# Experts' weights: four gate/up pieces of the next expert in a buffer of their own, copied into place, and 2 MB transfers

## The chip, the cores and the metric

The kernel runs on one core of a Trainium2 chip. The metric is the device time of one execution in microseconds, the median of several runs. All data is float32.

## The reference

Two layers of a network run on 512 tokens of width 1024. The first has a state-space mixer, a Fourier mixer and then a mixture of 32 experts, the second has attention, a gated recurrence and a dense feed-forward part. The change touches the experts alone:

```python
logits = (tok @ w_router + b_router)
top_logit, top_idx = lax.top_k(logits, TOP_K)            # 4 of 32 experts for each token
top_w = jax.nn.softmax(top_logit, axis=-1)
...
def expert_block(args):
    xe, e = args
    gu = xe @ w_gate_up[e] + b_gate_up[e]                # 1024 x 2048 for each expert: 8 MB
    gate = jnp.minimum(gu[:, :D_FF], SWIGLU_LIMIT)
    up = jnp.clip(gu[:, D_FF:], -SWIGLU_LIMIT, SWIGLU_LIMIT)
    act = (up + 1.0) * gate * jax.nn.sigmoid(SWIGLU_ALPHA * gate)
    return act @ w_down[e] + b_down[e]                   # 1024 x 1024 for each expert: 4 MB
```

Each token's four results are weighted by `top_w` and added. The 32 experts have 384 MB of weights, and each weight is needed once for each block of rows that its expert has.

## The kernel before

**Units.** The tokens of an expert are packed into units, which alternate between 32 rows (even units, `s = 0`) and 64 rows (odd units, `s = 1`). Two units make a turn of the loop (`PERIOD` = 96 rows). This input has 52 units in 26 turns, and an expert has one, two or three units, one after the other. Which expert a unit has is only known on the chip; a table `expert_of` says it (entry u + 1 for unit u, counted in the order in which the experts are worked off), and `first_unit` and `expert_at` give each expert's first unit and number.

**Weights.** Six slots of 16 KB in each partition hold one expert. A load is 1 MB (8 KB in each partition, half a slot). Gate/up weights are 16 pieces in 8 loads (slots 0 to 3), down weights are 8 pieces in 4 loads (slots 4 and 5). There is one semaphore for each of the 12 loads. There is no second copy: a half slot can be loaded again only when its last reader is through, and for an expert with several units that is in its last unit.

**SP (lines 1595 to 1605)** issues all these loads in one order. For each expert q with first unit u: eight gate/up loads, load i after piece 2i + 1 of unit u - 1; two small bias loads; four down loads, load i after down piece 2i + 1 in the turn of unit u (that product belongs to unit u - 1, see below). SP doesn't wait for a load to land; it waits only for the buffers.

**TensorE (lines 2752 to 2801)** does for each unit: gate/up pieces 0 to 7 (0 to 3 in a 64-row unit); transposes of the activations of the unit before (`turn_act`); pieces 8 and 9 (4 and 5); all eight down pieces of the unit before; the rest of the pieces, and in a 64-row unit transposes of the next tokens (`turn_x`) before piece 8 and at its end. Before each even piece it waits for the load that holds it.

**VectorE (lines 3721 to 3744)** waits for the biases of the unit, spreads them, waits for piece 15, and computes `gate`, `gate_min`, `up`, `up_clip`, `times` and `act`, with the sigmoid on ScalarE between. **GpSimd (lines 4110 to 4116)** once a turn waits for the end of the 64-row unit and gathers the rows of a later turn by an indirect DMA. **ScalarE** takes results out of PSUM and stores them.

`Steps` counts the steps of an engine on one semaphore: `at(name, u)` is its value once that step of unit u is done, `before(name, u)` that of unit u - 1.

Of the kernel before, what the change touches and what calls it, by code (L numbers as in the profile page):

```python
# [47 lines left out]
NE = 32  # L48
# [5 lines left out]
PART = D // TILES[0]  # L54
# [9 lines left out]
LOADS = GU_LOADS + DN_PIECES // 2  # L64
PIECE = 2 * 512
# [24 lines left out]
class Steps:  # L90
# [15 lines left out]
    def at(self, name, it=0):  # L106
        return it * self.n + (self.first + self.order.index(name) + 1)
# [45 lines left out]
def program(nc, io):  # L153
# [36 lines left out]
    def sem(name):  # L190
        return nc.alloc_semaphore(name)
# [10 lines left out]
    def row(w, i):  # L202
        return w[i] if isinstance(i, int) else w[bass.ds(i, 1)].rearrange("a p f -> p (a f)")
# [722 lines left out]
    def from_h(c, l, k):  # L926
# [127 lines left out]
                         "first_unit"] + [f"{n}{t}" for t in range(TT) for n in ("first_at", "first_pick")] + ["expert_of", "token_u", "y_row",  # L1054
# [9 lines left out]
    area = Area(AFTER_ROUTE, BACK_TABLES)  # L1064
# [3 lines left out]
    up = [area(f"up{s}", [P, s + 1, PART]) for s in range(2)]  # L1068
    sig = [area(f"sig{s}", [P, s + 1, PART]) for s in range(2)]
    aT = [area(f"aT{s}", [P, 2 * (s + 1), P]) for s in range(2)]  # L1070
    area = Area(AFTER_TABLES, AFTER_H)
    b_few = [area(f"b_few{s}", [P, s + 1, 2 * PART]) for s in range(2)]
    area = Area(AFTER_X1 + 36 * 1024)
    b_there = area("b_there", [P, 1])
    exp_loaded = w_loaded + [sem(f"exp_loaded{i}") for i in range(6, 18)]
    exp_first = loads + [0] * 12
# [7 lines left out]
    moe_xT_act = Steps(sem("moe_xT_act"), ["half0", "half1"], 1, ahead=True)  # L1084
    end_pe = Steps(sem("end_pe"), ["aT", "down"])
# [7 lines left out]
    AT_BANK, Y_BANK_OF = [3, 5], [7, 6]  # L1093
    s_gate_zero = sem("s_gate_zero")
# [362 lines left out]
    def _(sp):  # L1457
# [108 lines left out]
        def load_piece(i, e):  # L1566
            sp.dma_start(slot[i // 2][:, i % 2 * 2 * PIECE:(i % 2 + 1) * 2 * PIECE], row(io["w_exp"], e * LOADS + i)).then_inc(exp_loaded[i], 16)

# [5 lines left out]
        for i in range(GU_LOADS, LOADS):  # L1574
            load_piece(i, 0)
# [5 lines left out]
        for i in range(2, GU_LOADS):  # L1581
            load_piece(i, 0)
        sp.wait_ge(s_few, 2)
# [3 lines left out]
        moe_dn.open(sp)  # L1587
        route_dve.after(sp, "first_unit")
# [662 lines left out]
    def _(pe):  # L2251
# [500 lines left out]
        def turn(i, last_turn=False):  # L2752
            for s in range(2):
# [4 lines left out]
                def gate_up(pieces):  # L2758
                    for piece in pieces:
                        k, t = piece // 2, piece % 2  # L2760
                        if piece % 2 == 0:
                            pe.wait_ge(exp_loaded[piece // 2], e * 16 + (exp_first[piece // 2] + 16))
                        for h in range(2):
                            at = piece % 4 * PIECE + h * 512
                            half, tile = divmod(2 * t + h, TILES[s])
                            rows, first = UNIT_ROWS[s], UNIT_AT[s]
                            last = pe.matmul(GATE_PS[s][tile * rows:(tile + 1) * rows, half, :], xT_blk[:, k, first:first + rows],  # L2767
                                             slot[piece // 4][:, at:at + 512], start=(k == 0), stop=(k == KD - 1))
                        moe_gu.done(last, f"gu{piece}")
# [21 lines left out]
                for k in range(DN_PIECES):  # L2791
                    if k % 2 == 0:
                        pe.wait_ge(exp_loaded[GU_LOADS + k // 2], e_before * 16 + 16)
                    moe_dn.done(down(k, 1 - s), f"dn{k}")
# [301 lines left out]
    def _(dve):  # L3096
# [572 lines left out]
        step("y_row", dve.tensor_scalar(row_f[:], row_f[:], float(UNIT_ROWS[1]), None, ALU.add))  # L3669

# [19 lines left out]
        def last_rows(u):  # L3690
            last_dve.done(dve.tensor_scalar(last_from[:], n_started[:], -float(PERIOD), -float(UNIT_ROWS[1]), ALU.mult, ALU.add), "from")
# [29 lines left out]
        def turn(i, last=False):  # L3721
            for s in range(2):
# [7 lines left out]
                moe_dve.done(dve.stream_shuffle(b_row[s][:], b_few[s][:], [0] * 32), "spread")  # L3730
                dve.wait_ge(moe_dve.sem, moe_dve.at("spread", u))
# [12 lines left out]
                moe_dve.done(dve.tensor_tensor(gate[s][:], gate[s][:], sig[s][:], ALU.mult), "act")  # L3744

# [302 lines left out]
    def _(pool):  # L4048
# [60 lines left out]
        n = i_last + 1  # L4109
        with pool.Fori(0, i_last - 1) as i:  # L4110
# [5 lines left out]
            gather(token_now[:])  # L4116

# [3 lines left out]
        pool.wait_ge(exp_loaded[LOADS - 1], 16 * NE)  # L4121
# [144 lines left out]
def lay_out(x, c, ctx, c_ctx, w_mod, b_mod, norm1_w, norm2_w, w_in, conv_w, conv_b, dt_bias, a_log,  # L4266
# [58 lines left out]
    out["w_exp"] = np.concatenate([gu, dn], 1).reshape(NE * LOADS, P, 2 * PIECE)  # L4325
# [30 lines left out]
```

## Time and profile before

| what | value |
|---|---|
| median of 3 timed runs | 3032.16 us (3027.61 to 3032.35) |
| profiled execution, span | 3025.3 us; the profile gives no other time of it |
| TensorE matmuls busy | 2841.0 us, 94% |
| VectorE busy | 1377.2 us, 46% |
| ScalarE busy | 846.3 us, 28% |
| GpSimd busy | 303.8 us, 10% |
| read from HBM, written | 593.89 MB, 36.44 MB |
| expert weight loads | 384 of 1024 KB, median 11.4 us from issue to landing |
| expert stage (first to last of its TensorE work) | 992 to 2074 us |

In the page's 40 slices (75.6 us each) the experts are slices 14 to 28. There the DMA engines' digits are 8 and 9 and they move 310 to 411 GB/s, while TensorE's digits are 8 and 9 as in most of the span. A matmul counts as busy from its start to its modelled end, so TensorE's share says little about how near it is to its limit. The time from issue to landing of a load holds the time in which it stands behind others.

### The profile page before, as it was taken

To read this page: it belongs to the slowest core of one execution; us is meant where nothing else is said; L and a number is where in the kernel's file an instruction comes from. 1 tells how busy PE (TensorE), PEld (TensorE's weight loads), DVE (VectorE), ACT (ScalarE), POOL (GpSimd) and SP (SyncE) were. 2 spreads that over 40 slices of the span, in tenths; PEclk is the share of its full clock that TensorE was granted. 3 is DMA by queue.
4 is the path that set the end of the run, shared out by engine and by line. 5 is a ranking of instruction groups with operands and counts; after the bars stand their busy time and mean duration, and the time that the engine had idled before them with its cause. 6 is when DMAs were issued, how large, how long until landed. Compare 5 with 4: busy or idle time off the path is not lost.

```text
span 3025.3 us, 41220 instructions
## 1 busy us (share of the span) xinstructions
PE 2841.0 (94%) x15088; PEld 1753.1 (58%) x15089; DVE 1377.2 (46%) x2323; ACT 846.3 (28%) x1661; POOL 303.8 (10%) x291
## 2 busy tenths in 40 slices
PE   8999999999999978888989898879999999999999
PEld 5665656746888422222323232226877888888887
DVE  5768678644455211112112121124674786555551
ACT  4547365501212211111211121113243544211100
POOL 0101011310001000000000000003111553000000
PEclk9999999999999988999989998989999999999999
DMA  5433425355124899979798989997120222122111
GB/s 226 160 112 132 150 95 205 154 199 194 67 89 166 337 410 405 409 316 402 313 404 348 387 328 410 411 411 290 56 115 17 92 81 98 35 89 86 61 65 60
DMA packets 137826, 634.03 MB, mean 210 GB/s; under 512 B 12848, under 2 KB 55728, under 8 KB 77040
## 3 DMA queue, kind: packets, MB, share of 16 engines
q1 hardware_dynamic: 110832, 562.65, 47.3%
q0 software_dynamic: 10112, 35.66, 3.6%
q10 hardware_dynamic: 16768, 34.17, 3.1%
q8 instruction: 76, 1.25, 0.2%
q14 instruction: 38, 0.31, 0.0%
HBM read 593.89 MB, written 36.44 MB: 208 GB/s over the span
## 4 chain that ended last, share of the span: by engine, by line
PE 79%; DMA 10%; DVE 4%; ACT 3%; issue 2%; POOL 1%; SPq 0%; ACTq 0%; DVEq 0%; POOLq 0%
PE ps L340 27%; PE ps L2767 17%; PE ps L2747 9%; PE ps L2317 9%; DMA slot<-in_w_exp 8%; PE ps L279 3%; PE ps L2464 2%; DMA w_modT<-in_w_modT 2%; PE ps L3030 2%; PE ps L2473 2%; PE ps L3002 1%; PE ps L2738 1%; PE ps L2985 1%; PE ps L2256 1%; ACT decay L1818 1%
## 5 line engine op out<-in xcount | busy, mean ns | idle before, releaser
L2767 PE MATMUL ps<-slot,xT_blk 128*32 128x512 f32 (+1 forms) x3328 | 615.7, 638 | 137.7 <-DMA slot<-in_w_exp 137.3
L2767 PEld LDWEIGHTS ps<-slot,xT_blk 128*32 128x32 f32 (+1 forms) x3328 | 159.3, 128 | 497.3 <-issue 307.5
L2747 PE MATMUL ps<-slot,aT 128*32 128x256 f32 (+1 forms) x2528 | 286.5, 454 | 0.0
L3729 DVE MEMSET b_there<- 128x1 f32 x52 | 3.1, 59 | 494.7 <-DMA b_few<-in_b_gu 482.2
L2747 PEld LDWEIGHTS ps<-slot,aT 128*32 128x32 f32 (+1 forms) x2528 | 111.3, 119 | 183.8 <-issue 152.4
L3733 DVE TENSOR_TENSOR gate<-ps,b_row 128x256 f32<-128x256 f32 (+1 forms) x52 | 29.0, 558 | 344.1 <-PE ps L2767 344.1
L340 PE MATMUL ps<-in_t,in_s 128*128 128x264 f32 x528 | 124.8, 387 | 0.5 <-issue 0.5
L2464 PE MATMUL ps<-hT,slot 128*128 128x512 f32 x256 | 120.7, 604 | 2.2 <-ACT zT L1763 2.1
L2317 PE MATMUL ps<-h_sum,w_sum 128*128 128x384 f32 (+1 forms) x384 | 120.2, 460 | 0.0
L1980 ACT ACTIVATE y_row<-ps 128x512 f32<-128x512 f32 (+1 forms) x52 | 25.5, 490 | 333.2 <-PE ps L2747 333.2
L340 PEld LDWEIGHTS ps<-in_t,in_s 128*128 128x128 f32 x528 | 100.5, 190 | 17.8 <-DVE in_s L429 0.9
L279 PE MATMUL ps<-gate_yT,slot 128*128 128x512 f32 x256 | 110.0, 593 | 0.0
L1983 ACT ACTIVATE aT<-ps 128x512 f32<-128x512 f32 (+1 forms) x53 | 26.1, 492 | 272.9 <-PE ps L2738 272.9
L2317 PEld LDWEIGHTS ps<-h_sum,w_sum 128*128 128x128 f32 x384 | 72.5, 190 | 40.1 <-issue 1.9
L3231 DVE SCALAR_TENSOR_TENSOR conv_b<-raw,g_conv,conv_b 128x510 f32<-128x510 f32 (+1 forms) x112 | 66.8, 633 | 46.7 <-ACT conv_b L1736 45.6
L340 PE MATMUL ps<-xnT,in_w 128*128 128x264 f32 x352 | 85.5, 387 | 0.0
L279 PEld LDWEIGHTS ps<-gate_yT,slot 128*128 128x128 f32 x256 | 48.8, 191 | 60.7 <-issue 59.4
L2004 ACT ACTIVATE sig<-gate 128x256 f32<-128x256 f32 (+1 forms) x52 | 27.2, 523 | 195.7 <-DVE gate L3735 195.6
L1818 ACT ACTIVATE decay<-sum_here,g_small 128x128 f32<-128x128 f32 x256 | 78.1, 387 | 13.6 <-PE ps L2473 13.6
L2317 PE MATMUL ps<-hT,slot 128*128 128x384 f32 (+1 forms) x256 | 81.1, 462 | 0.0
L4115 POOL TENSOR_TENSOR token_there<-cst 128x1 f32<-128x1 f32 x24 | 4.6, 192 | 755.0 <-PE ps L2733 755.0
L279 PE MATMUL ps<-xnT,slot 128*128 128x264 f32 x352 | 80.3, 386 | 0.0
(572 smaller groups left out, 4984.9 us busy)
## 6 DMA issues: line engine op xcount, KB each, us to landing
slot<-in_w_exp SPq DMA_DIRECT2D x384, 1024.0 KB, 11.4
in_w<-in_w_ffn SPq DMA_DIRECT2D x22, 1024.0 KB, 4.8
expert_rows<-zero SPq DMA_DIRECT2D x4, 4608.0 KB, 24.3
slot<-in_w_xbc SPq DMA_DIRECT2D x8, 2048.0 KB, 8.2
sum_here<-sum_rows ACTq DMA_DIRECT2D x32, 512.0 KB, 3.7
w_modT<-in_w_modT POOLq DMA_DIRECT2D x32, 512.0 KB, 3.9
rnn_w<-in_w_rnn SPq DMA_DIRECT2D x16, 1024.0 KB, 4.9
out_w<-in_w_ffn_out SPq DMA_DIRECT2D x8, 1408.0 KB, 7.5
```

Source lines behind the costliest of these rows:

```text
L279: last = pe.matmul(self.bank(j, part), self.layout(slot[s], m, k), self.rhs(k, part), start=(k == 0), stop=(k == self.k - 1))
L340: last = pe.matmul(like(out, right), lhs[:, k, :], right, start=(start and k == 0), stop=(k == self.kh - 1), skip_group_check=not start)
L1818: last = act.activation(decay[j % 2][:, h, :], sum_here[j % 2][:, h, :], ACT.Abs, bias=g_small[:, MINUS_SUM, t, d, h:h + 1])
L2256: pe.matmul(ps[:, bank, 0:256], ident, cst[:, 0:256], start=True, stop=True)
L2317: last = pe.matmul(out, left[:, k, :], right(k), start=(start and k == 0), stop=(k == KD // 2 - 1), skip_group_check=not start)
L2464: last = pe.matmul(ps[:, 3, :], slot[SSD_SLOT[s, "z"][0]][:, (k * 4 + m) * P:(k * 4 + m + 1) * P], hT[:, k, 0:SEQ], start=(k == 0), stop=( ...
L2473: last = pe.matmul(ps[half, Y_BANK + h // 2, t * P:(t + 1) * P], left[:, h * HD:(h + 1) * HD], right[:, h, :], start=first, stop=True, ski ...
L2738: last = pe.transpose(ps[:, AT_BANK[s], c * P:(c + 1) * P], acts[:, c * P:(c + 1) * P], ident)
L2747: last = pe.matmul(ps[j * rows:(j + 1) * rows, Y_BANK_OF[s], 0:width], aT[s][:, 2 * half + c, tile * rows:(tile + 1) * rows], slot[4 + k / ...
L2767: last = pe.matmul(GATE_PS[s][tile * rows:(tile + 1) * rows, half, :], xT_blk[:, k, first:first + rows], slot[piece // 4][:, at:at + 512], ...
L3030: last = pe.matmul(ps[:, 2 * (j % 4) + p, 0:H2], slot[j // 4][:, (k * 4 + j % 4) * P:(k * 4 + j % 4 + 1) * P], attnT[:, k, p * H2:(p + 1) ...
L3231: last = dve.scalar_tensor_tensor(out=acc[:, lo:hi], in0=raw_tile(m)[:, lo + off:hi + off], scalar=g_conv[:, m, k:k + 1], in1=acc[:, lo:hi ...
```

## The change

- A new area of 32 KB in each partition at the top of SBUF (`AHEAD_AT`) holds the last four gate/up loads (4 to 7, pieces 8 to 15, 4 MB) of the next expert. Slots 2 and 3 hold those of the present expert, as before. Several small buffers move to make room. `span` is one tensor from slot 2 to the end of SBUF, so that source and place are offsets in it.
- At the end of each unit these four are copied to slots 2 and 3 for the next unit: from the new area if the next unit has another expert, else onto themselves (`held_from` is the offset, `TO_AHEAD` or 0). VectorE does this behind `act` of the unit: copies 4 to 7 after a 32-row unit, 5 to 7 after a 64-row unit. There GpSimd does copy 4, after piece 9 of that unit. A copy is 128x2048 elements.
- TensorE waits for the copies instead of loads 4 to 7.
- SP's order for each expert: gate/up loads 0 to 3 and the biases as before; wait for copies 4 and 5 of its first unit, then loads 4 and 5 of the next expert in one transfer of 2 MB; wait for copy 7, then loads 6 and 7 in another; then the down weights in two transfers of 2 MB, after down pieces 3 and 7. The second expert's four start after the first piece of unit 0.
- Weights in HBM lie in two tensors, 1 MB rows for loads 0 to 3, 2 MB rows for the others. Three small instructions in the routing make `held_from`. Semaphores of the later layers are numbered anew.

```diff
+        def load_pair(i, e, at=0):
+            into = span[:, at + (i - 4) * 2 * PIECE:at + (i - 2) * 2 * PIECE] if i < GU_LOADS else slot[i // 2][:]
+            sp.dma_start(into, row(io["w_two"], e * (LOADS // 2 - 2) + (i // 2 - 2))).then_inc(exp_loaded[i], 16)
...
-        with sp.Fori(1, NE) as q:
-            u = sp.value_load(first_unit[0:1, bass.ds(q, 1)], min_val=1, max_val=UNITS)
-            e = sp.value_load(expert_at[0:1, bass.ds(q, 1)], min_val=0, max_val=NE - 1)
-            for i in range(GU_LOADS):
+        def load_gate_up(e, u):
+            for i in range(GU_LOADS - AHEAD):
                 sp.wait_ge(moe_gu.sem, moe_gu.before(f"gu{2 * i + 1}", u))
                 load_piece(i, e)
             sp.wait_ge(moe_dve.sem, moe_dve.before("spread", u))
             load_bias(e)
-            for i in range(DN_PIECES // 2):
-                sp.wait_ge(moe_dn.sem, moe_dn.before(f"dn{2 * i + 1}", u + 1))
-                load_piece(GU_LOADS + i, e)
+
+        def load_down(e, u):
+            for i in range(0, DN_PIECES // 2, 2):
+                sp.wait_ge(moe_dn.sem, moe_dn.before(f"dn{2 * i + 3}", u + 1))
+                load_pair(GU_LOADS + i, e)
+
+        e_first = sp.value_load(expert_at[0:1, 1:2], min_val=0, max_val=NE - 1)
+        moe_gu.after(sp, "gu0")
+        for i in range(GU_LOADS - AHEAD, GU_LOADS, 2):
+            load_pair(i, e_first, TO_AHEAD)
+        with sp.Fori(1, NE - 1) as q:
...
+            load_gate_up(e, u)
+            sp.wait_ge(moe_copy4.sem, moe_copy4.before("copy4", u))
+            sp.wait_ge(moe_copies.sem, moe_copies.before("copy5", u))
+            load_pair(4, e_next, TO_AHEAD)
+            sp.wait_ge(moe_copies.sem, moe_copies.before("copy7", u))
+            load_pair(6, e_next, TO_AHEAD)
+            load_down(e, u)
...
@@ TensorE, gate_up
-                        if piece % 2 == 0:
+                        if piece % 2 == 0 and piece < 2 * (GU_LOADS - AHEAD):
                             pe.wait_ge(exp_loaded[piece // 2], e * 16 + (exp_first[piece // 2] + 16))
+                        elif piece == 8:
+                            pe.wait_ge(moe_copy4.sem, moe_copy4.before("copy4", u))
+                        elif piece % 2 == 0:
+                            pe.wait_ge(moe_copies.sem, moe_copies.before(f"copy{piece // 2}", u))
...
@@ VectorE, behind "act"
+                if more:
+                    for k in range(s, AHEAD):
+                        dve.wait_ge(exp_loaded[landed(4 + k)], e_next * 16 + (exp_first[landed(4 + k)] + 16))
+                        copied = dve.tensor_copy(held(k), span[:, bass.ds(from_at + k * 2 * PIECE, 2 * PIECE)])
...
@@ GpSimd
+        def copy_4(i):
+            u = 2 * i + 2
...
+            pool.wait_ge(moe_gu.sem, moe_gu.at("gu9", u - 1))
+            pool.wait_ge(exp_loaded[4], e * 16 + (exp_first[4] + 16))
+            moe_copy4.done(pool.tensor_copy(held(0), span[:, bass.ds(from_at, 2 * PIECE)]), "copy4")
...
             pool.tensor_copy(token_now[:], token_u[:, bass.ds(i + 2, 1)]).then_inc(s_now, 1)
+            copy_4(i)
             pool.wait_ge(moe_xT_pe.sem, moe_xT_pe.at("half1", i))
```

## Rows read from the trace of the kernel before

**Rows 1.** The page's costliest group: busy, mean ns | idle before it, releaser.

```profile
L2767 PE MATMUL ps<-slot,xT_blk 128*32 128x512 f32 (+1 forms) x3328 | 615.7, 638 | 137.7 <-DMA slot<-in_w_exp 137.3
```

**Rows 2.** Windows: busy us by engine (instructions), PEclk, DMA share, GB/s.

```profile
992.00:2074.00 1082.00, 943.93 (x6244) 310.45 (x6244) 213.38 (x485) 192.96 (x411) 37.59 (x76) 0.92 0.95 380
1093.00:1107.00 14.00, 8.92 (x30) 2.56 (x34) 0.00 (x0) 0.38 (x1) 0.00 (x0) 0.61 1.02 424
1322.00:1337.00 15.00, 15.00 (x132) 5.85 (x128) 2.14 (x4) 2.49 (x9) 1.19 (x2) 1.00 0.04 9
1438.00:1453.00 15.00, 15.00 (x128) 5.77 (x124) 2.21 (x5) 2.64 (x10) 1.27 (x2) 1.00 0.03 9
1654.00:1664.00 10.00, 10.00 (x60) 3.04 (x58) 1.97 (x6) 2.30 (x3) 0.18 (x1) 1.00 0.12 26
1766.00:1777.00 11.00, 11.00 (x64) 3.32 (x62) 2.04 (x6) 2.30 (x3) 0.18 (x1) 1.00 0.11 25
```

**Rows 3.** Timeline of SP, expert stage: start, length, issues merged.

```profile
993.48 14.21 SPq L1567 DMA_DIRECT2D slot<-in_w_exp  x8
1014.16 27.67 SPq L1567 DMA_DIRECT2D slot<-in_w_exp  x12
1048.30 12.27 SPq L1567 DMA_DIRECT2D slot<-in_w_exp  x12
1178.05 26.97 SPq L1567 DMA_DIRECT2D slot<-in_w_exp  x12
1308.24 42.38 SPq L1567 DMA_DIRECT2D slot<-in_w_exp  x12
1634.59 46.41 SPq L1567 DMA_DIRECT2D slot<-in_w_exp  x12
```

**Rows 4.** Chain of work, two units and the last load: start, length.

```profile
1397.98 19.72 DMA slot<-in_w_exp
1435.72 1.87 PE ps L2767 x8
1437.59 3.59 PE ps L2747 x64
1443.53 7.02 PE ps L2767 x32
1451.02 3.57 PE ps L2767 x32
2053.47 16.10 DMA slot<-in_w_exp
```

**Rows 5.** Timeline of DVE, "gate" and "act" of three units.

```profile
1431.86 0.42 DVE L3733 TENSOR_TENSOR gate<-ps,b_row 128x256 f32<-128x256 f32 x1 [2.63 <-PE ps L2767]
1450.59 0.69 DVE L3733 TENSOR_TENSOR gate<-ps,b_row 128x512 f32<-128x512 f32 x1 [14.44 <-PE ps L2767]
1453.66 0.69 DVE L3744 TENSOR_TENSOR gate<-gate,sig 128x512 f32<-128x512 f32 x1
1466.00 0.42 DVE L3733 TENSOR_TENSOR gate<-ps,b_row 128x256 f32<-128x256 f32 x1 [10.33 <-PE ps L2767]
1468.01 0.42 DVE L3744 TENSOR_TENSOR gate<-gate,sig 128x256 f32<-128x256 f32 x1
```

**Rows 6.** Groups of DVE by shape: busy us, mean ns | idle before.

```profile
L3738 DVE TENSOR_SCALAR up<-up 128x512 f32<-128x512 f32 x26 | 11.5, 443 | 0.9
L3738 DVE TENSOR_SCALAR up<-up 128x256 f32<-128x256 f32 x26 | 7.6, 294 | 0.9
```

**Rows 7.** The same view of GpSimd.

```profile
L4066 POOL TENSOR_TENSOR x_dt<-x_tok,g_small 128x2048 f32<-128x2048 f32 x4 | 15.8, 3952 | 52.6 <-PE ps L2473 52.6
L4100 POOL MEMSET b_few<- 128x1024 f32 x1 | 1.0, 952 | 0.0
```

**Rows 8.** DMA issues: count, KB each, median us to landing.

```profile
in_w<-in_w_ffn SPq DMA_DIRECT2D x22, 1024.0 KB, 4.8
slot<-in_w_gf SPq DMA_DIRECT2D x2, 2048.0 KB, 7.9
```

More of the change, by code:

```diff
@@ L1063, in program @@
     y_row = [area(f"y_row{s}", [P, s + 1, PART]) for s in range(2)]
-    area = Area(AFTER_ROUTE, BACK_TABLES)
+    up = [area(f"up{s}", [P, s + 1, PART]) for s in range(2)]
+    sig = [area(f"sig{s}", [P, s + 1, PART]) for s in range(2)]
+    assert area.next <= STAGE + KD * SEQ * 4
+    area = Area(AFTER_H, AFTER_ROUTE)
     b_row = [area(f"b_row{s}", [P, s + 1, 2 * PART]) for s in range(2)]
@@ L1067, in program, with landed @@
     gate = [area(f"gate{s}", [P, s + 1, PART]) for s in range(2)]
-    up = [area(f"up{s}", [P, s + 1, PART]) for s in range(2)]
-    sig = [area(f"sig{s}", [P, s + 1, PART]) for s in range(2)]
     aT = [area(f"aT{s}", [P, 2 * (s + 1), P]) for s in range(2)]
+    meta_x = area("meta_x", [P, KD, N_META])
+    square_meta = area("square_meta", [P, KD, N_META])
+    b_there = area("b_there", [P, 1])
+    AHEAD_AT = END // 32 * 32 - AHEAD * SLOT_BYTES // 2
+    assert area.next <= AHEAD_AT
+    area = Area(AHEAD_AT)
+    area.next += AHEAD * SLOT_BYTES // 2
+    assert area.next <= END
+    HELD_AT = FREE + (GU_LOADS - AHEAD) * SLOT_BYTES // 2
+    span = at("span", [P, (END // 32 * 32 - HELD_AT) // 4], HELD_AT)
+    TO_AHEAD = (AHEAD_AT - HELD_AT) // 4
     area = Area(AFTER_TABLES, AFTER_H)
     b_few = [area(f"b_few{s}", [P, s + 1, 2 * PART]) for s in range(2)]
[L1073 to L1076, printed above, removed]
+    exp_loaded = w_loaded + [sem(f"exp_loaded{i}") for i in range(6, 16)]
+    exp_first = loads + [0] * 10
+    def landed(piece):
+        return piece if piece < GU_LOADS - AHEAD else piece - piece % 2
     TURN_AT, DOWN_AT = [8, 4], [10, 6]
@@ L1093, in program, with held @@
     AT_BANK, Y_BANK_OF = [3, 5], [7, 6]
+    def held(k, at=0):
+        return span[:, at + k * 2 * PIECE:at + (k + 1) * 2 * PIECE]
     s_gate_zero = sem("s_gate_zero")
@@ L1573, in _ @@
         four_out.pe.all(sp)
-        for i in range(GU_LOADS, LOADS):
-            load_piece(i, 0)
+        for i in range(GU_LOADS, LOADS, 2):
+            load_pair(i, 0)
         w_o.pe.after(sp, "p4_1")
@@ L2760, in gate_up @@
                         k, t = piece // 2, piece % 2
-                        if piece % 2 == 0:
+                        if piece % 2 == 0 and piece < 2 * (GU_LOADS - AHEAD):
                             pe.wait_ge(exp_loaded[piece // 2], e * 16 + (exp_first[piece // 2] + 16))
+                        elif piece == 8:
+                            pe.wait_ge(moe_copy4.sem, moe_copy4.before("copy4", u))
+                        elif piece % 2 == 0:
+                            pe.wait_ge(moe_copies.sem, moe_copies.before(f"copy{piece // 2}", u))
                         for h in range(2):
                             at = piece % 4 * PIECE + h * 512
+                            weights = slot[piece // 4]
+                            if piece >= 2 * (GU_LOADS - AHEAD):
+                                weights, at = span, at + (piece // 4 * 4 - 2 * (GU_LOADS - AHEAD)) * PIECE
                             half, tile = divmod(2 * t + h, TILES[s])
@@ L2767, in gate_up @@
                             last = pe.matmul(GATE_PS[s][tile * rows:(tile + 1) * rows, half, :], xT_blk[:, k, first:first + rows],
-                                             slot[piece // 4][:, at:at + 512], start=(k == 0), stop=(k == KD - 1))
+                                             weights[:, at:at + 512], start=(k == 0), stop=(k == KD - 1))
                         moe_gu.done(last, f"gu{piece}")
@@ L2801, in turn @@
                     gate_up(range(DOWN_AT[s], GU_PIECES))
+        for i in range(GU_LOADS - AHEAD, GU_LOADS, 2):
+            pe.wait_ge(exp_loaded[i], exp_first[i] + 16)
         with pe.Fori(0, i_last) as i:
@@ L3730, in turn @@
                 moe_dve.done(dve.stream_shuffle(b_row[s][:], b_few[s][:], [0] * 32), "spread")
+                more = not (s and last)
+                if more:
+                    e_next = dve.value_load(expert_of[0:1, bass.ds(u + 2, 1)], min_val=0, max_val=NE - 1)
+                    from_at = dve.value_load(held_from[0:1, bass.ds(u + 1, 1)], min_val=0, max_val=TO_AHEAD)
                 dve.wait_ge(moe_dve.sem, moe_dve.at("spread", u))
@@ L3744, in turn @@
                 moe_dve.done(dve.tensor_tensor(gate[s][:], gate[s][:], sig[s][:], ALU.mult), "act")
+                if more:
+                    for k in range(s, AHEAD):
+                        dve.wait_ge(exp_loaded[landed(4 + k)], e_next * 16 + (exp_first[landed(4 + k)] + 16))
+                        copied = dve.tensor_copy(held(k), span[:, bass.ds(from_at + k * 2 * PIECE, 2 * PIECE)])
+                        if k == 0:
+                            moe_copy4.done(copied, "copy4")
+                        else:
+                            moe_copies.done(copied, f"copy{4 + k}")
         with dve.Fori(0, i_last) as i:
```

58 lines of the change are left out of this document (41 added, 17 removed).

## The prediction

> **What bounds the kernel now.** I read the page first: TensorE matmuls are busy 94% of the span, and the costliest group of waits behind them is on the expert weights, 137 us of idle TensorE before the gate/up matmuls [rows 1]. So the stage to look at is the experts', 992 to 2074 us. The windows view tells which resource is full there [rows 2]: over the whole stage the DMA engines are busy 0.95 of the time at 380 GB/s; where TensorE waits for weights (1093 to 1107) they stand at 1.02 and 424 GB/s, which is as full as they get, with transfers of 1 MB. A transfer of 1 MB (1.049 MB in bytes) then takes 2.47 us. The stage is bound by DMA, and TensorE's waits are the consequence. What can be won is only the time in which the DMA engines stand idle, and that is in four places: 15, 15, 10 and 11 us, together 51 us, at a share of 0.03 to 0.12 [rows 2].
>
> The SP queue's timeline says why just there [rows 3]. A burst of 12 issues is four down loads of one expert, then eight gate/up loads of the next, which wait for that expert's last unit. Its length gives the expert's units: 12 to 14 us is one unit (14 such bursts), 27 us two units (26.97 for the 3 that begin on a 32-row unit, 27.67 for the 9 that begin on a 64-row unit), 42.38 or 46.41 us three units (2 and 2). The four idle places lie in the four three-unit bursts. Two-unit experts leave the DMA engines no idle time now, because the eight gate/up loads of the next expert are released one by one all through the last unit.
>
> **The DMA ledger of before.** First issue 993.48, last landing 2053.47 + 16.10 = 2069.57 [rows 3, 4]: 1076.1 us for 31 experts. Off this go the 51 us idle and four restarts of 2.3 us (a lone 1 MB load lands after 4.8 us [rows 8], 2.47 are its bytes): 60 us. What is left is 1016 us, so D = 32.8 us for the 12 MB of an expert, the stores and gathers that share the engines included.
>
> **What the change does to the queue.** Order on SP for an expert e with first unit u becomes: gate/up loads 0 to 3 of e (released in unit u-1, as now); then the wait for copy 4 and 5 of unit u and a 2 MB load of the next expert's pieces, the wait for copy 7 and the second 2 MB; then the down weights in two 2 MB loads. The copies of unit u run on VectorE behind "act" of unit u-1, that is after the last matmul of u-1 and the whole SwiGLU chain. So for each expert all traffic stops at one point until the previous expert's last unit is computed, evaluated and copied. Before, no such point existed: gate/up loads 4 to 7 needed only the piece of the slot they fill. Between two such points lie exactly 12 MB. Call T the landing of gate/up load 3 of e. Behind T the queue holds 12 MB more (ahead pieces, down, next loads 0 to 3), so the DMA engines run dry at T + 32.8. The next issue comes at T + TensorE's way to the end of e's last unit + the VectorE chain + one copy (5; after a 64-row unit GpSimd does copy 4) or two (4 and 5).
>
> Terms, all from rows:
> - TensorE. In the trace a load 3 lands at 1397.98 + 19.72 = 1417.70, and the two units behind it (32, then 64 rows) end at 1450.55 [rows 4]: 32.8 us; the first alone ends near 1431.8, 14.1 us. Each further unit is read off the "gate" instructions that wait for a unit's end, at 1431.86, 1450.59, 1466.00 [rows 5]: 18.7 us for 64 rows, 15.4 for 32. An expert that begins on a 64-row unit needs load 2 (T - 2.5) for pieces 4 and 5, and from there to the unit's end it is 1450.55 - 1435.72 = 14.8 [rows 4]: T + 12.3.
> - VectorE chain: 1466.00 to 1468.43 is 2.4 us; 1450.59 to 1454.35 is 3.8 us [rows 5].
> - A copy of 128x2048 on VectorE is not in the trace. The one-source operation takes 294 ns for 256 and 443 ns for 512 elements [rows 6], a slope of 0.58 ns: 1.3 us. The two-source one ("gate", 0.42 and 0.69 us [rows 5]) has 1.06 ns: 2.3 us. The copy has one source in SBUF and so has the first; I take 1.3. Below, nothing; above, 2.3.
> - Restart of an empty queue with a 2 MB load: 7.9 us lone [rows 8] less 4.9 for its bytes, 3.0 us. Bounds 1.5 (half of it hidden) and 3.3.
>
> Idle time per expert (path less 32.8):
> - one unit: 14.1 + 2.4 + 2.6 + 3.0 = 22.1, below 32.8: none.
> - two units, 32 rows first: 32.8 + 3.8 + 1.3 + 3.0 = 40.9: 8.1 us, x3 = 24.
> - two units, 64 rows first: 12.3 + 15.4 + 2.4 + 2.6 + 3.0 = 35.7: 2.9 us, x9 = 26.
> - three units, 32 rows first: 14.1 + 18.7 + 15.4 + 2.4 + 2.6 + 3.0 = 56.2: 23.4 us, x2 = 47.
> - three units, 64 rows first: 12.3 + 15.4 + 18.7 + 3.8 + 1.3 + 3.0 = 54.5: 21.7 us, x2 = 43.
>
> Together 140 us idle against 60 before: +80. About 5 us come back, since stores and gathers, which D holds as a share, now move some of their bytes in idle time. The sum is +75 us.
>
> **The other parts.** VectorE's copies delay TensorE nowhere while their weights are there: after a 32-row unit they end 2.4 + 5.2 = 7.6 us on, while the next unit reaches piece 8 after pieces 0 to 7, down and transposes, about 11.7 us [rows 4]; after a 64-row unit three end 3.8 + 3.9 = 7.7 us on and piece 10 comes after 12.7 us. Behind the copies on VectorE stand the bias spread (0.7 to 1.3 us) and the next "gate", 15 us away. At 2.3 us a copy piece 8 still gets copy 4 in time. GpSimd's copy 4 starts at piece 9 of the 64-row unit, 5.3 us before its end, and is bounded by 1.0 us (memset, 1024 elements) and 3.95 us (two sources, 2048 elements) [rows 7]; it is off the path either way. The gather behind it on GpSimd waits for the unit's end anyway. Transfers of 2 MB instead of two of 1 MB: bytes and the rate are the same, zero; SP issues 8 instead of 12 loads, each far shorter than its transfer, zero. The start: the first expert's ahead pieces load from 992.6 on instead of 993.5, zero, but put 10 us before the loads of unit 1, which belongs to the 12 MB cycles already counted. Three routing instructions of some 0.2 us: nothing.
>
> A lone load shows a fixed part of 2.3 us for 1 MB, and full windows of 1 MB loads show none [rows 2, 8]. The Trainium skill (DMA: Bandwidth & Descriptors, section Anatomy of one DMA) gives about 2.0 us plus bytes over 436 GB/s for a transfer (fitted on the GpSimd path), 4.4 us for this one, and by it larger transfers pay. If each transfer of a full queue cost its 2.0 us, four fewer for each of 31 experts would save 248 us, an estimate from that page; the 424 GB/s of 1 MB loads speak against it.
>
> **The sum.** The profile has a span of 3025.3 us and gives no time of its own around it; the timed runs, 3027.6 to 3032.4, lie 2 to 7 us above it. The stage grows from 1082 to 1157 us, all else stays: 3025 + 75 = 3100 in span, 3032 + 75 = 3107 us in the median.
>
> **Rivals.**
> - Faster: the prefetch closes the four idle places and opens none. All 60 us come back: 2972. It decides at the point where the issue waits for copies end before the queue is dry, a path below 32.8 us for two-unit experts: the 64-row-first ones miss it by 2.9, which a restart hidden behind the running transfer would give back, the 32-row-first ones by 8.1; the three-unit ones can't reach it, since one expert's 12 MB is all that the buffers take. For it: the slots' wait does start 4 MB earlier in a long expert. Against: the same 12 MB lie between two waits. 0.09.
> - Full queues gain from fewer, larger transfers, 2.0 us for each of 124: 3107 - 248 = 2859, faster; for it only the lone load's fixed part, against it [rows 2]. 0.02.
> - The loss is small: two-unit experts lose nothing, because their next issue is hidden behind the running transfers, and a restart costs 1.5. Then the three-unit experts idle 90 - 6 = 84 us against 60, +24: 3056; with stores and gathers filling all of that, 3032. 0.07, half of it within 0.2%.
> - Copies at 2.3 us: 3 + 18 + 4 + 2 = 27 copies lie on the path, +27: 3134. By the skill (SBUF — State Buffer, section SBUF: two separate sides) VectorE in a two-port mode and GpSimd exclude each other for whole instructions; no row shows them together, and it would act in the same direction. 0.17.
> - The forecast, 3107: 0.65.
>
> **Range and chances.** Low end: 3 us off each of 16 restarts (48) is 3059, and the small loss ends at 3056: 3055. High end: copies at 2.3 and the low clock after longer waits, about 1 us on each of the 16 (a 32-row unit's transposes and pieces 8, 9 take longer behind the wait): 3150. Slower by over 0.2% (6 us, what a measurement can tell): 0.65 + 0.17 + 0.035 = 0.855, within 0.2%: 0.03, faster: 0.115.
>
> **What would show it.** In the changed profile: SP waits for VectorE's copies, longest in two-unit experts that begin with 32 rows and in three-unit experts; DMA share of the stage about 0.89 instead of 0.95, with gaps ahead of the ahead pieces of some 3, 8 and 22 us; VectorE copies near 1.3 us; TensorE still waiting on DMA at the first piece of an expert, and almost never on a copy. I am wrong if the share rises, if SP's wait for the copies ends before the queue is dry, or if 12 MB take clearly more or less than 32.8 us.

## The result

The changed kernel takes 3104.5 us (median of 4 runs, 3101.2 to 3107.2) against 3029.9 us before in the same comparison: a ratio of 1.0251, 95% interval 1.0236 to 1.0267 (the record's own; the quotient of the two medians would be 1.0246). It is slower by 2.5%; the forecast was 3107, the range 3055 to 3150. The profiled execution took 3104.6 us with a span of 3102.8 us, 77.5 more than before's span.

The page of the kernel after (groups: busy us, mean ns | idle before, releaser; DMA issues: count, KB, median us to landing). The one group of [rows 1] is now two, since pieces 8 to 15 are read through `span`:

```profile
L2821 PE MATMUL ps<-slot,xT_blk 128*32 128x512 f32 (+1 forms) x1664 | 331.4, 671 | 208.3 <-DMA slot<-in_w_exp 207.9
L2794 PE MATMUL ps<-slot,aT 128*32 128x256 f32 (+1 forms) x2528 | 288.8, 455 | 8.1 <-DMA slot<-in_w_two 8.0
L2821 PE MATMUL ps<-span,xT_blk 128*32 128x512 f32 (+1 forms) x1664 | 286.2, 602 | 0.0
L3812 DVE COPY span<-span 128x2048 f32 x179 | 207.5, 1219 | 0.0
L4189 POOL COPY span<-span 128x2048 f32 x25 | 47.2, 1890 | 727.9 <-PE ps L2821 727.9
slot<-in_w_exp SPq DMA_DIRECT2D x128, 1024.0 KB, 14.0
span<-in_w_two SPq DMA_DIRECT2D x64, 2048.0 KB, 10.7
```

TensorE's idle time for gate/up weights rose from 137.7 [rows 1] to 208.3 us, and 8.1 us for down weights are new: together 79 us, about what the span grew by. It never waits for a copy (0.0 before the `span` matmuls). The VectorE copies cost 207.5 us of VectorE's time, most of it beside other work.

The windows view of the kernel after (columns as in [rows 2]; the five engines are TensorE, its weight loads, VectorE, ScalarE and GpSimd). I call a stop a stretch in which the queue has run dry, or nearly, and the next load is still held back, and I call experts 32-first or 64-first by the rows of their first unit. The rows are the whole expert stage, a stretch in which TensorE waits, then a stop in an expert of two units beginning with 64 rows, one in an expert of two beginning with 32, one in an expert of three beginning with 32 and one in an expert of three beginning with 64, and the last expert:

```profile
994.00:2157.00 1163.00, 946.40 (x6244) 309.52 (x6236) 414.03 (x663) 194.14 (x412) 90.84 (x105) 0.90 0.89 355
1106.00:1120.00 14.00, 7.99 (x34) 2.41 (x38) 3.40 (x6) 0.38 (x1) 0.00 (x0) 0.65 1.01 424
1050.00:1060.00 10.00, 10.00 (x98) 3.96 (x96) 6.12 (x8) 1.18 (x4) 0.00 (x0) 1.00 0.68 250
1218.00:1232.00 14.00, 14.00 (x90) 4.58 (x88) 7.59 (x12) 3.44 (x7) 1.76 (x3) 1.00 0.54 188
1345.00:1386.00 41.00, 40.71 (x318) 14.20 (x314) 19.55 (x31) 7.95 (x18) 3.33 (x4) 1.00 0.51 187
1703.00:1742.00 39.00, 37.29 (x254) 12.46 (x252) 15.93 (x26) 7.53 (x16) 3.83 (x5) 1.00 0.55 184
2126.00:2150.00 24.00, 23.39 (x158) 10.32 (x154) 7.99 (x16) 2.46 (x5) 2.11 (x2) 0.93 0.61 238
```

The same view of the kernel before, wider than in [rows 2] so that the restarts are inside: one of the two stops of each kind, and the last expert. (The page's DMA digits of the slices 14 to 28 there are 7 to 9, at 290 to 411 GB/s, and not only 8 and 9; the 7s of slices 18 and 20, at 316 and 313 GB/s, are two of these stops.)

```profile
1318.00:1345.00 27.00, 27.00 (x196) 9.55 (x194) 6.07 (x13) 5.23 (x13) 1.44 (x3) 1.00 0.42 154
1650.00:1668.00 18.00, 18.00 (x110) 5.59 (x110) 4.46 (x13) 3.70 (x6) 0.18 (x1) 1.00 0.33 105
2050.00:2072.00 22.00, 21.38 (x158) 10.05 (x148) 6.15 (x14) 3.85 (x7) 1.87 (x2) 1.00 0.84 339
```

The stage grew from 1082 to 1163 us, and its share fell from 0.95 to 0.89, while a full stretch still moves 424 GB/s. So the loss is time in which DMA doesn't run at that rate, and a window tells how much: its length times (1 - GB/s / 424). That holds idle time and restart together, as the terms of the forecast did. Before, the four stops lose 17.2, 16.9, 13.5 and 12.8 us, 60 in all. After:

| stop | count | one, lost us | all | forecast |
|---|---|---|---|---|
| one unit | 14 | none seen | 0 | 0 |
| two units, 64 rows first | 9 | 3.3 to 4.7 | 36 | 26 |
| two units, 32 rows first | 3 | 7.8, 7.2, 7.4 | 22 | 24 |
| three units, 32 rows first | 2 | 22.9, 22.9 | 46 | 47 |
| three units, 64 rows first | 2 | 22.1, 22.2 | 44 | 43 |
| last expert (before 4.4) | 1 | 10.5 | +6 | 0 |

The stops lose 148 us, 88 more than before; with the last expert 94. The stage shows 81, so 13 us come back in stores and gathers that now move in idle time.

The place of a stop is seen in three views of the kernel after, here for the expert of two units that begins with 32 rows. The chain of work (start, length):

```profile
1162.49 25.41 DMA slot<-in_w_exp
1199.12 10.27 DMA slot<-in_w_two
1213.72 7.02 PE ps L2821 x32
```

The timelines of VectorE and of SP behind it:

```profile
1220.79 0.69 DVE L3797 TENSOR_TENSOR gate<-ps,b_row 128x512 f32<-128x512 f32 x1 [10.81 <-PE ps L2821]
1223.87 0.69 DVE L3808 TENSOR_TENSOR gate<-gate,sig 128x512 f32<-128x512 f32 x1
1224.47 3.49 DVE L3812 COPY span<-span 128x2048 f32 x3
1225.87 2.61 SPq L1590 DMA_DIRECT2D span<-in_w_two  x2
```

Load 3 lands at 1187.90 (1162.49 + 25.41). The last unit of its expert ends at 1220.74, 32.8 us on. VectorE evaluates until 1224.47, the first copy ends near 1225.7, and SP issues the first ahead load at 1225.87 and the second after copy 7, some 2.3 us later (the row's 2.61 us run to the end of the second issue). The queue had held 12 MB behind load 3 and ran empty at the same time (the first of these windows; the other two belong to the expert of three units at 1345):

```profile
1219.00:1226.00 7.00, 7.00 (x58) 2.17 (x52) 4.97 (x8) 3.42 (x7) 1.27 (x2) 1.00 0.21 69
1348.00:1363.00 15.00, 14.71 (x116) 5.22 (x112) 3.77 (x6) 3.22 (x11) 3.15 (x3) 1.00 0.08 16
1376.00:1381.00 5.00, 5.00 (x24) 1.41 (x20) 4.79 (x8) 0.81 (x3) 0.00 (x0) 1.00 0.01 2
```

SP's waits (in all us, count, the longest) name who holds it. By its releasers L1644 is the wait for copy 4; the waits for copies 5 and 7 are counted at the issues, L1590:

```profile
SPq L1644 <- DVE span L3812: 120.9, 12, 11.8
SPq L1590 <- DVE span L3812: 156.9, 60, 7.9
SPq L1644 <- POOL span L4189: 11.6, 5, 2.3
```

### The profile page after: what moved, and what is told of

Read it like the earlier page. It is cut to its first block, busy times and chain, and to the rows that moved or that the text cites. A ratio compares the mean times of both kernels' runs of the same rounds, so it can differ in the third digit from the quotient of the medians.

```text
span 3102.8 us, 41967 instructions
## 1 busy us (share of the span) xinstructions
PE 2842.4 (92%) x15088; PEld 1747.3 (56%) x15089; DVE 1577.7 (51%) x2505; ACT 846.4 (27%) x1661; POOL 352.0 (11%) x317
## 4 chain that ended last, share of the span: by engine, by line
PE 76%; DMA 15%; DVE 3%; ACT 2%; issue 2%; SPq 1%; POOL 1%; ACTq 0%; DVEq 0%; POOLq 0%
PE ps L341 26%; PE ps L2821 13%; DMA slot<-in_w_exp 9%; PE ps L2364 9%; PE ps L2794 8%; PE ps L280 6%; DMA slot<-in_w_two 4%; PE ps L2511 2%; PE ps L3086 2%; PE ps L2520 2%; PE ps L3058 1%; PE ps L3041 1%; DMA slot<-in_w_mod 1%; PE ps L2785 1%; ACT decay L1865 1%
## 5 line engine op out<-in xcount | busy, mean ns | idle before, releaser
L2821 PE MATMUL ps<-slot,xT_blk 128*32 128x512 f32 (+1 forms) x1664 | 331.4, 671 | 208.3 <-DMA slot<-in_w_exp 207.9
L2821 PEld LDWEIGHTS ps<-slot,xT_blk 128*32 128x32 f32 (+1 forms) x1664 | 79.9, 131 | 404.0 <-DMA slot<-in_w_exp 254.9
L2821 PE MATMUL ps<-span,xT_blk 128*32 128x512 f32 (+1 forms) x1664 | 286.2, 602 | 0.0
L3812 DVE COPY span<-span 128x2048 f32 x179 | 207.5, 1219 | 0.0
L2821 PEld LDWEIGHTS ps<-span,xT_blk 128*32 128x32 f32 (+1 forms) x1664 | 79.4, 123 | 164.8 <-issue 161.9
L4189 POOL COPY span<-span 128x2048 f32 x25 | 47.2, 1890 | 727.9 <-PE ps L2821 727.9
```

The costliest lines, as they stand in the source:

```text
L3812: copied = dve.tensor_copy(held(k), span[:, bass.ds(from_at + k * 2 * PIECE, 2 * PIECE)])
L4189: moe_copy4.done(pool.tensor_copy(held(0), span[:, bass.ds(from_at, 2 * PIECE)]), "copy4")
```

## The experiments

Each is an edit of the kernel after, but for the one that says so. Times are medians, the ratio is to the kernel before in the same comparison.

**The copies' length.** In e2 VectorE's copies move 32 columns instead of 2048.

```diff
-copied = dve.tensor_copy(held(k), span[:, bass.ds(from_at + k * 2 * PIECE, 2 * PIECE)])
+copied = dve.tensor_copy(held(k)[:, 0:32], span[:, bass.ds(from_at + k * 2 * PIECE, 32)])
```

> The changed kernel with VectorE's copies cut to 32 columns each (so pieces 8 to 15 of later experts are multiplied mostly with old weights; GpSimd's copy stays whole): all waits and their places remain, only the length of a copy goes from 1.22 us to about 0.1. Theory A: 27 copies lie on the paths that empty the queue, 27 x 1.1 = 30 us less than the changed kernel: 3070 to 3080. Theory C (VectorE's 208 us of copies are the loss): all 75 us back, 3030. If copies are hidden altogether: 3104.

Measured: 3074.35 us, 1.0147 (1.0130 to 1.0164), in the range. The group of copies:

```profile
L3812 DVE COPY span<-span 128x32 f32 x179 | 22.9, 176 | 0.4 <-issue 0.4
```

Each is 1.04 us shorter (1.219 - 0.176). Pieces 8 to 15 of later experts are multiplied mostly with old weights. The forecast's 27 copies on the path make 28 us; the ratio fell by 0.0104, 31 us of 3030. Of 76 us lost (0.0251), 31 are the copies' own length. The other 45 stay although the copies take almost no time.

**The copies twice.** In e3b a second pass, times 1.0, follows each of VectorE's copies 5 to 7, and the waits are for that.

```diff
+moe_copies.done(copied, f"first{4 + k}")
+dve.wait_ge(moe_copies.sem, moe_copies.at(f"first{4 + k}", u))
+moe_copies.done(dve.tensor_scalar(held(k), held(k), 1.0, None, ALU.mult), f"copy{4 + k}")
```

> The changed kernel, and behind each of VectorE's copies 5, 6 and 7 a second pass over the copied 128x2048 in place (times 1.0), so that copy 5, 6 and 7 each take twice as long; copy 4 once. Theory A: one doubled copy, copy 5, lies ahead of the first ahead load in each of the 16 experts with two or three units, 16 x 1.3 = 21 us more: 3118 to 3132; the doubled 6 and 7 end within the 5 us that the first 2 MB take. Theory C (the loss goes with VectorE's busy time): 150 more passes of 1.2 us, 60 us more or all 180: 3165 and up. If copies are hidden: 3104.

Measured: 3146.54 us, 1.0398 (1.0380 to 1.0415): 0.0147 or 44 us above the kernel after. Both numbers of the expectation missed; mine, 3118 to 3132, counted one pass more at each of 16 stops. The windows and SP's timeline of this kernel, for the stops at 1345 and 1703 of the kernel after and the issue at 1225.87:

```profile
1353.00:1394.00 41.00, 40.99 (x317) 14.41 (x318) 29.56 (x37) 8.30 (x18) 4.42 (x4) 1.00 0.48 173
1728.00:1770.00 42.00, 38.75 (x252) 12.74 (x250) 24.12 (x33) 7.53 (x16) 4.02 (x5) 0.96 0.48 162
1229.32 5.13 SPq L1590 DMA_DIRECT2D span<-in_w_two  x2
```

These two stops lose 24.3 and 26.0 us instead of 22.9 and 22.1. SP's timeline tells where all of the 44 us are. The ahead loads before and at one 64-first stop, first in the kernel after and then in this one:

```profile
1241.08 2.61 SPq L1590 DMA_DIRECT2D span<-in_w_two  x2
1292.80 2.61 SPq L1590 DMA_DIRECT2D span<-in_w_two  x2
```

```profile
1244.53 5.28 SPq L1590 DMA_DIRECT2D span<-in_w_two  x2
1299.96 5.13 SPq L1590 DMA_DIRECT2D span<-in_w_two  x2
```

From one to the other it is 51.7 us in the kernel after and 55.4 here. Taken for all 16 stops, these stretches are longer by 24 us (nine 64-first experts of two units), 8 (three 32-first) and 12 (four of three units), 44 in all. One pass at each stop is in it as counted: the first ahead load comes 4.9 or 5.1 us behind the last unit's "gate" in the kernel after and 6.1 to 6.4 here, some 20 us in all. The other 24 arise behind the first ahead load, where the expectation had nothing. My reading, not tested by itself: the two ahead loads are now issued over 5.13 us, against 2.61. In the kernel after the second is in the queue well before the bytes of the first (4.9 us) are through; here it comes about as they end, so the passes between copies 5 and 7 count as well.

**The copies' place.** In e5 VectorE makes copies 4 to 6 ahead of the unit's SwiGLU, after pieces 9, 11 and 13 of its last unit have been read; only copy 7 stays behind `act`. The same copies and transfers.

```diff
+for k in range(s, AHEAD - 1):
+    dve.wait_ge(moe_gu.sem, moe_gu.at(f"gu{9 + 2 * k}", u))
+    copy(k)
...
-    for k in range(s, AHEAD):
+    copy(AHEAD - 1)
```

> The changed kernel with VectorE's copies 4, 5 and 6 moved ahead of the SwiGLU chain, each as soon as its pieces are through (pieces 9, 11, 13); copy 7 stays behind 'act'. Theory A (the DMA queue runs dry because the next ahead load waits for last unit + VectorE chain + copy): the paths get 6 to 7 us shorter, the gaps of two-unit experts go, those of three-unit experts shrink by 5 to 7: 50 to 74 us back, 3030 to 3055 us. Theory B (the loss is the size and order of the transfers, not the wait): about 3104. Theory C (VectorE's copies themselves are in the way of the work): no gain, since as many copies run, or worse, because they now stand ahead of the activation: 3104 or more.

Measured: 3050.25 us, 1.0079 (1.0062 to 1.0096), in the range of the first theory. VectorE's timeline and SP's waits of this kernel:

```profile
1206.65 1.25 DVE L3798 COPY span<-span 128x2048 f32 x1 [10.05 <-PE ps L2821]
1208.35 1.23 DVE L3798 COPY span<-span 128x2048 f32 x1 [0.45 <-PE ps L2821]
1209.87 0.69 DVE L3810 TENSOR_TENSOR gate<-ps,b_row 128x512 f32<-128x512 f32 x1 [0.29 <-PE ps L2821]
SPq L1644 <- DVE span L3798: 5.8, 12, 2.1
SPq L1590 <- DVE span L3798: 219.4, 48, 7.5
```

Two copies are done ahead of "gate" at 1209.87. SP's wait for copy 4, 120.9 us, is down to 5.8. Those for copies 5 and 7 rise from 156.9 to 219.4 us, since copy 7 still stands behind `act` and is now what SP stands at. Together they fall by 53 us, and 52 of the 76 us are back with every copy still made. So it is shown that the place of the copies behind SwiGLU is the larger part of the loss.

**The transfers' size.** e8 leaves the copies late and makes all loads 1 MB, each behind its own copy; e7 has early copies and 1 MB loads; e1 is the kernel before with the down weights in 2 MB loads.

```diff
-into = span[:, at + (i - 4) * 2 * PIECE:at + (i - 2) * 2 * PIECE] if i < GU_LOADS else slot[i // 2][:]
-sp.dma_start(into, row(io["w_two"], ...)).then_inc(exp_loaded[i], 16)
+for j in (i, i + 1):
+    wait(j)
+    into = held(j - 4, at) if j < GU_LOADS else slot[j // 2][:, j % 2 * 2 * PIECE:(j % 2 + 1) * 2 * PIECE]
+    sp.dma_start(into, row(io["w_two"], e * (LOADS - 4) + (j - 4))).then_inc(exp_loaded[j], 16)
```

> The changed kernel, copies where the change put them, but all loads of 1 MB, each released by its own copy or down pieces. With the run of early copies and 1 MB loads (ratio 1.0018) and early copies and 2 MB loads (1.0079) it makes the fourth corner. Theory A: the late place of the copies is the larger part and the 2 MB grain the smaller, and a late copy costs less where copy 4 alone releases the first load: 35 to 60 us above the kernel before, 3060 to 3090. If the grain matters only beside late copies: under 3050.

> The early copies as in the other run, and all loads of 1 MB again, each released by its own copy or down pieces. Theory A with grains (a 2 MB load is released by the later of its two halves and lands as a whole, some 2.5 us each time where the queue is near dry): 10 to 20 us below the early copies with 2 MB loads, 3025 to 3045. If the size of a transfer in a queue that is mostly full is nothing: the same as the early copies within 5 us.

The edit of e1, in the kernel before:

```diff
-for i in range(DN_PIECES // 2):
-    sp.wait_ge(moe_dn.sem, moe_dn.before(f"dn{2 * i + 1}", u + 1))
-    load_piece(GU_LOADS + i, e)
+for i in range(0, DN_PIECES // 2, 2):
+    sp.wait_ge(moe_dn.sem, moe_dn.before(f"dn{2 * i + 3}", u + 1))
+    load_pair(GU_LOADS + i, e)
```

> The kernel before with one part of the change alone: the down weights in two transfers of 2 MB instead of four of 1 MB, gate/up loads as before, no new buffer and no copies. If each transfer of a full queue had a fixed cost of 2.0 us (the Trainium skill, DMA: Bandwidth & Descriptors, section Anatomy of one DMA), 62 fewer would save 124 us: 2903. Theory A (no fixed cost in a full queue; a 2 MB load is released later and lands as a whole): the same to 12 us slower, 3027 to 3040. Theory B (the size is what costs the changed kernel its time): half or more of the 75 us, 3060 and up.

Measured: e8 3076.82 us, 1.0161 (1.0144 to 1.0178); e7 3033.91, 1.0018 (1.0008 to 1.0027); e1 3033.28, 1.0016 (1.0006 to 1.0025). All three are in their ranges. With the kernel after and e5 that gives, as loss against before:

| | 2 MB | 1 MB |
|---|---|---|
| copies behind `act` | +76 us | +49 us |
| copies 4 to 6 ahead of it | +24 us | +5 us |

(the ratio less 1, times 3030; by the intervals each is good to 3 to 5 us). The place is worth 52 and 43 us, the size 27 and 19, which is too near to call them different. The size is no cost of the transfer: 64 large ones for 128 small ones cost 5 us in before's order. What differs is the wait: the first ahead load in e8 waits for copy 4 alone. That is one copy less behind `act` of a 32-row unit, and behind a 64-row unit none of VectorE's, since GpSimd makes copy 4 during that unit. The windows of e8 at a 32-first and a 64-first stop:

```profile
1218.00:1232.00 14.00, 13.00 (x84) 3.72 (x76) 6.32 (x11) 4.31 (x7) 0.50 (x2) 1.00 0.82 321
1285.00:1301.00 16.00, 14.16 (x116) 5.40 (x112) 5.38 (x9) 2.50 (x9) 3.10 (x3) 1.00 0.99 407
```

They lose 3.4 and 0.6 us, against 7.8 and 3.8 in the kernel after.

**What the ahead area is worth.** In e4 there are no copies: SP waits only for the landing of the previous ahead load and TensorE for the landings. The values of pieces 8 to 15 are therefore not the right ones; traffic and matmuls are the same. e9 is that with 1 MB loads.

```diff
-sp.wait_ge(moe_copy4.sem, moe_copy4.before("copy4", u))
-sp.wait_ge(moe_copies.sem, moe_copies.before("copy5", u))
+sp.wait_ge(exp_loaded[4], q * 16 + (exp_first[4] + 16))
 load_pair(4, e_next, TO_AHEAD)
-sp.wait_ge(moe_copies.sem, moe_copies.before("copy7", u))
+sp.wait_ge(exp_loaded[6], q * 16 + (exp_first[6] + 16))
 load_pair(6, e_next, TO_AHEAD)
```

> The changed kernel without any copy (its gate/up pieces 8 to 15 are multiplied with the first expert's weights that stay in place; this is the part of the computation that it changes); TensorE waits for the landing of each expert's ahead loads instead, and SP issues the next ones as soon as the previous ones have landed, without waiting for a unit's end. All bytes are loaded in the same transfers and order. Theory A: the gaps behind units go, what is left are the waits for slots in three-unit experts, as before the change, and 2 MB grains: 3035 to 3055. If loading 4 MB ahead wins by itself and only the copies spoil it: under 3000. Theory B (size and order of transfers): still near 3100.

> As the run without copies (pieces 8 to 15 always with the first expert's weights in place, SP never waits for a unit's end ahead of the ahead loads), and all loads of 1 MB. It is the bound of what 4 MB more of look-ahead can give in this order of loads. The run without copies and with 2 MB loads had a ratio of 1.0024, and 1 MB loads took 0.0061 to 0.0090 off in the two pairs of runs; so if the grain is the rest of its loss: 0.994 to 0.998, 3010 to 3022 us, 4 MB of look-ahead are worth 6 to 18 us and the copies with early places eat them. If look-ahead is worth nothing here (the three-unit gaps keep their length, the last expert has nothing behind it): 1.000 to 1.002.

Measured: e4 3035.44 us, 1.0024 (1.0014 to 1.0034), at the low end of its range and not under 3000, where look-ahead would have brought it. e9 3033.26 us, 1.0010 (1.0001 to 1.0019), the expectation for an area worth nothing. So the area alone, with copies that cost nothing, saves nothing. The windows of e9, a three-unit expert and the last one:

```profile
1328.00:1343.00 15.00, 15.00 (x128) 5.79 (x124) 2.02 (x4) 2.33 (x8) 1.03 (x2) 1.00 0.04 9
2050.00:2076.00 26.00, 25.38 (x162) 10.84 (x160) 6.17 (x14) 2.52 (x6) 2.32 (x2) 0.89 0.64 248
```

The gap of 15 us in a three-unit expert stands as in [rows 2] (0.04, 9 GB/s), and so do the other three, at shares of 0.04, 0.14 and 0.24. Loads 0 to 3 still have to wait until the slots are free in the expert's last unit. My reading of it, from the order and not tested by itself: the queue behind load 3 is 4 MB longer, but the first unit can now be finished when load 3 is there and not load 7, also 4 MB earlier, so the two cancel. The traces agree. VectorE's timeline, the "gate" that waits for the end of that first unit, in the kernel before and in e9:

```profile
1316.01 0.42 DVE L3733 TENSOR_TENSOR gate<-ps,b_row 128x256 f32<-128x256 f32 x1 [2.42 <-PE ps L2767]
1322.18 0.42 DVE L3805 TENSOR_TENSOR gate<-ps,b_row 128x256 f32<-128x256 f32 x1 [13.05 <-PE ps L2819]
```

The gap begins near 1322 before and near 1328 in e9: both times 6 us behind this point. And the last expert has no ahead loads behind it: that window loses 10.8 us, in before 4.4.

**Another order.** In e6 the down weights stand ahead of the ahead pieces.

```diff
 load_gate_up(e, u)
+load_down(e, u)
 sp.wait_ge(moe_copy4.sem, moe_copy4.before("copy4", u))
...
-load_down(e, u)
```

> The changed kernel with the down weights of an expert loaded ahead of the next expert's ahead pieces. Theory A: SP's stop is then at down piece 3 of the expert's first unit, which comes 3 to 7 us later than the copies, and with it the ahead loads' stop: each of the 31 experts' cycles can only get longer, 3150 to 3210. Rival (the ahead pieces delay weights that are needed sooner, the down weights that TensorE waits for): down weights come earlier, 3060 to 3095.

Measured: 3206.53 us, 1.0593 (1.0575 to 1.0611), in the range. TensorE's group and SP's wait of this kernel:

```profile
L2821 PE MATMUL ps<-slot,xT_blk 128*32 128x512 f32 (+1 forms) x1664 | 343.1, 693 | 305.3 <-DMA slot<-in_w_exp 304.8 <-issue 0.4
SPq L1590 <- PE ps L2794: 752.5, 62, 34.2
```

The down slots are free later than the copies are made, and all that stands behind the down loads in the queue waits with them: 305 us of idle TensorE, against 208 in the kernel after. Which waiting load stands first decides more here than how much buffer there is.

No version beats the kernel before. The nearest, e9, e1 and e7, are 0.10, 0.16 and 0.18% above it.

## Why the prediction was right, step by step

- **Bound by DMA.** Right: share 0.89 as forecast, TensorE busy 943.9 [rows 2] and 946.4 us in the stage, its waits up by 79 us, and the rate of a full stretch unchanged at 424.
- **One stop per expert, 12 MB between two.** Right. SP stands at L1644 and L1590 on VectorE's copies (the first ahead load comes 4.9 us behind the "gate" of a 32-row unit and 5.1 us behind that of a 64-row unit; the forecast had 5.0 and 5.1), and e5 takes away 52 us by moving them. T + 32.8 for both the end of two units and the dry queue held where I looked (1220.7 and the window from 1219).
- **The stops' lengths.** 148 us against 140. The 64-first experts of two units lose 4.0 instead of 2.9 us each, +10 in all; the others are within 1 to 2 us as groups. The term that was too small is the first 64-row unit, T + 12.3. In six of the nine its "gate" comes at T + 13.3 to 14.2, together some 9 us more. TensorE's timeline at pieces 0 to 3 of such an expert (its T is 1259.0) and of one whose weights were there at once; then two windows of the first:

```profile
1251.51 5.75 PE L2821 MATMUL ps<-slot,xT_blk 128*64 128x512 f32 x16 [15.41 <-DMA slot<-in_w_exp]
1375.23 3.65 PE L2821 MATMUL ps<-slot,xT_blk 128*64 128x512 f32 x16
```

```profile
1252.00:1255.00 3.00, 3.00 (x10) 0.73 (x8) 0.00 (x0) 0.00 (x0) 0.00 (x0) 0.50 1.01 426
1257.00:1260.00 3.00, 3.00 (x24) 1.08 (x26) 0.55 (x3) 0.38 (x1) 0.00 (x0) 1.00 1.08 442
```

Behind a wait of 15.41 us TensorE's granted clock is 0.50 (1.2 GHz) from 1252 to 1255, and 1.00 (2.4 GHz) from 1257 on. The 16 matmuls of these pieces take 5.75 us instead of 3.65 (there at a clock of 1.00), so pieces 4 and 5 start 1.1 us behind the time of load 2, T - 2.5, at which I had them. In a seventh expert (load 0 read at 1011.06, after a wait of 2.41 us) the clock is 1.00 and the "gate" comes at T + 12.3. The prediction had the low clock only in its high end, as 1 us at each of 16.
- **Right in part by luck.** In the other two of the nine, and in both 64-first experts of three units, load 3 lands 2 to 4 us ahead of the stop before, so the queue was dry once more behind T. Their last "gate" comes at T + 35.4 and 35.8 instead of 27.7, and at T + 51.7 and 52.2 instead of 46.4. What holds for them is the 12 MB between two stops (1380.28 + 3.0 + 32.8 is 1416.1, the next issue comes at 1416.19). That they lose 3.3, 3.4, 22.1 and 22.2 us, near the forecast, is no merit of its path.
- **Where in a three-unit expert.** The sum was right, its picture was not. I had one gap of 22 us ahead of the ahead pieces. The trace has two: 1348 to 1363 (share 0.08) ahead of loads 0 to 3, as before, and 1376 to 1381 (share 0.01) ahead of the ahead pieces. The loads 0 to 3 between them move 4 MB that I had put behind one gap; the path between two stops is the same, so the sum is.
- **Not in the forecast.** The last expert (+6 us), and TensorE's waits for down weights that now stand behind the ahead loads in the queue (8.0 us, part of a DMA bound time, so not an addition). Against these, stores and gathers give back 13 us and not 5, a term that I had put in without rows. The three misses, +8 for the stops, +6 and -8, leave the stage 6 us above the forecast (1163 against 1157). The rest of the span, for which I had no change, is 4 us shorter (1939.8 against 1943.3), and the kernel before took 3029.9 us in the comparison, not 3032. That 3107 meets 3104.5 so closely is luck; the terms are good to some 10 us.
- **Copies 1.3 us, behind which TensorE never waits.** Right: 1.219 us and 0.0. The rival at 2.3 us falls. GpSimd's 1.89 us lies inside its bounds of 1.0 and 3.95 [rows 7] and off the path. The Trainium skill (VectorE: DVE Perf Modes, section The perf-mode tier table) has 1227 ns for an fp32 copy of 2048 elements in SBUF, since one source may use both ports, and the trace agrees with 1219.
- **2 MB cost zero.** As a price of the transfer right (5 us for 64, e1); as a part of this change it hid in two of my terms, the restart (3.0 against 2.3) and two copies ahead of the first load. 16 x 0.7 + 11 x 1.2 make 24 of the 140 us, against 27 measured. It should have stood by itself, since it is the one part that could be left out alone.
- **The rival of a fixed 2.0 us per transfer** falls: e1 sends 64 transfers fewer (62 of them in this stage) and is 0.16% slower. By the Trainium skill (DMA: Bandwidth & Descriptors, section Anatomy of one DMA, a fit to the GpSimd path) 62 fewer would be 124 us, an estimate; no run here shows that in a full queue.
- **The faster rival** (no wait left before the queue is dry) fails, and e9 says more: with the wait gone wholly the four gaps stay as they were. I had given this rival 60 us of gain; even its ideal form has none. That was wrong in my text, and it did not change the sum.

## What to carry to other kernels

When a stage is bound by DMA, only the idle time of the engines can be won: find those gaps, and ask of a new buffer whether the load behind the gap can start earlier, not whether some load can. SP issues its loads in one order, so a wait put on one load is a wait on all behind it (e6: 305 us of idle TensorE against 208): release it by the earliest work that frees the place, ahead of the evaluation chain, and per piece and not per pair. Work out bytes between two stops against the time between their releases; that gave the growth of the stage here to 6 us, with misses of 8, 6 and 8 us in its terms.

## What I had not expected of the hardware

**GpSimd's copy is held up by VectorE's.** In e6 both wait for the same landing and start together. The timelines of GpSimd and VectorE there:

```profile
1074.00 2.97 POOL L4189 COPY span<-span 128x2048 f32 x1 [31.63 <-DMA span<-in_w_two]
1140.86 1.89 POOL L4189 COPY span<-span 128x2048 f32 x1 [54.16 <-PE ps L2821]
1073.99 1.23 DVE L3812 COPY span<-span 128x2048 f32 x1 [3.25 <-DMA span<-in_w_two]
```

Alone GpSimd takes 1.89 us, beside VectorE 2.97 (2.96 or 2.97 in all 7 such cases), while VectorE's stays at 1.23: 1.08 us more, most of VectorE's copy. That agrees with the rule of the Trainium skill (SBUF — State Buffer, section SBUF: two separate sides) that one of the two has the shared ports for a whole instruction. In the kernel after they don't meet: GpSimd copies at 1215.85, five microseconds ahead of VectorE's chain.

**Where the grain matters.** A full stretch of 1 MB loads moves 424 GB/s [rows 2]. A window of the kernel after behind the landing of a load 3 at 1259.0, where the two ahead loads of 2 MB are next in the queue:

```profile
1259.50:1268.50 9.00, 9.00 (x92) 3.89 (x94) 1.31 (x2) 1.42 (x5) 0.93 (x1) 1.00 1.01 428
```

That is the same rate. Yet the size is worth 27 us with late copies and 19 with early ones, where each stop waits for two halves and must be restarted, and 5 us for the down weights alone.
